# Weight splits rounded in two halves, the second output slab's split moved behind the differential attention, first scores in the free accumulator pair, one join's squares moved ahead

## The reference, cut to what matters

```python
log_a = jax.nn.log_sigmoid((ar @ w_a2 + b_a)) / GLA_TAU
oa = gla(aq, ak, av, log_a)
oa = rmsnorm(oa, gla_gain) * jax.nn.silu(ag)
bq, bk = rmsnorm(bq, dq_gain), rmsnorm(bk, dk_gain)
ob = diff_attention(bq, bk, bv, lam)      # (softmax(q1 k1') - lam softmax(q2 k2')) v, causal
ob = rmsnorm(ob, diff_gain) * (1.0 - lambda_init)
x = x + concat(oa, ob) @ w_out
x = x + conv_ffn(rmsnorm(x, g), w_up, conv_w, conv_b, w_down)
```

## Time and profile before

| | us |
|---|---|
| median of 3 runs | 3355.73 |
| lowest, highest | 3351.95, 3360.63 |
| the profiled execution's own time | 3357.11 |
| its span in the trace | 3355.3 |
| PE busy in the span | 3278.1 (98%) |
| DVE, ACT, POOL busy | 1809.4 (54%), 1247.2 (37%), 1020.4 (30%) |
| granted TensorE clock, mean | 0.995 |

### The profile page before, as it was taken

The page is one execution under the profiler, slowest core; times in us unless marked ns, Lnnn a source line. Parts: engine busy times, 40 slices in busy tenths (PEclk is TensorE's granted clock), DMA queues, the critical chain, the costliest instruction groups (busy, mean ns, idle before and its releaser), DMA issues.

```text
span 3355.3 us, 48284 instructions
## 1 busy us (share of the span) xinstructions
PE 3278.1 (98%) x17840; PEld 2804.2 (84%) x17840; DVE 1809.4 (54%) x2219; ACT 1247.2 (37%) x1627; POOL 1020.4 (30%) x505
## 2 busy tenths in 40 slices
PE   7989999999999999999999999999999999999999
PEld 6768888888888888998888877988888888998887
DVE  5467876553478766457645665664552255262222
ACT  4464333354444334443322445322242223442221
POOL 2112222221112222544434241343423332223332
PEclk9999999999999999999999999999999999999999
DMA  4202333321224333445544310454422243222222
GB/s 143 73 37 101 144 138 125 113 102 51 88 84 156 136 133 109 174 174 185 186 155 175 120 67 14 156 189 150 169 101 100 93 164 113 95 82 100 100 89 100
DMA packets 69901, 401.69 MB, mean 120 GB/s; under 512 B 7520, under 2 KB 10224, under 8 KB 31216
## 3 DMA queue, kind: packets, MB, share of 16 engines
q1 hardware_dynamic: 46400, 317.80, 26.2%
q10 hardware_dynamic: 23344, 81.73, 6.9%
HBM read 397.41 MB, written 2.10 MB: 119 GB/s over the span
## 4 chain that ended last, share of the span: by engine, by line
PE 90%; DVE 3%; ACT 3%; issue 2%; POOL 1%; DMA 1%; SPq 0%; DVEq 0%; ACTq 0%; POOLq 0%
PE banks L535 24%; PE banks L537 23%; PE banks L536 23%; PE banks L441 3%; PE banks L442 3%; PE banks L443 3%; PE banks L552 2%; PE banks L554 2%; PE banks L553 2%; ACT whi L970 1%; POOL wlo L2262 1%; PE banks L651 1%; DMA raw<-stream 1%; PE banks L886 1%; PE banks L873 1%
## 5 line engine op out<-in xcount | busy, mean ns | idle before, releaser
L2262 POOL TENSOR_TENSOR wlo<-raw,whi 128x512 fp32r<-128x512 f32 (+1 forms) x282 | 707.7, 2510 | 2025.7 <-ACT whi L970 2023.7
L535 PE MATMUL banks<-h_hi,whi 128*128 128x512 f32 (+1 forms) x2752 | 1040.2, 378 | 11.5 <-POOL wlo L2262 5.4
L536 PE MATMUL banks<-h_lo,whi 128*128 128x512 f32 (+1 forms) x2752 | 1034.2, 376 | 0.0
L537 PE MATMUL banks<-h_hi,wlo 128*128 128x512 f32 (+1 forms) x2752 | 1034.2, 376 | 0.0
L970 ACT ACTIVATE whi<-raw 128x2048 fp32r<-128x2048 f32 x281 | 536.9, 1911 | 527.8 <-PE banks L537 523.1
L1524 DVE TENSOR_TENSOR wlo<-raw,whi 128x1536 fp32r<-128x1536 f32 (+1 forms) x281 | 530.6, 1888 | 296.2 <-ACT whi L970 296.0
L535 PEld LDWEIGHTS banks<-h_hi,whi 128*128 128x128 f32 x2752 | 518.3, 188 | 112.2 <-issue 16.3
L536 PEld LDWEIGHTS banks<-h_lo,whi 128*128 128x128 f32 x2752 | 518.5, 188 | 94.3 <-issue 1.7
L537 PEld LDWEIGHTS banks<-h_hi,wlo 128*128 128x128 f32 x2752 | 518.5, 188 | 94.0
L535 PE MATMUL banks<-mid_hi,whi 128*128 128x512 f32 (+1 forms) x1136 | 424.6, 374 | 4.0 <-POOL wlo L2262 3.1
L536 PE MATMUL banks<-mid_lo,whi 128*128 128x512 f32 (+1 forms) x1136 | 424.0, 373 | 0.0
(11 more groups left out here) (287 smaller groups left out, 4029.6 us busy)
## 6 DMA issues: line engine op xcount, KB each, us to landing
raw<-stream SPq DMA_DIRECT2D x298, 1024.0 KB, 4.8
mraw<-mod_stream ACTq DMA_DIRECT2D x144, 512.0 KB, 3.4
x<-xT SPq DMA_DIRECT2D x8, 256.0 KB, 6.1
out<-x SPq DMA_DIRECT2D x8, 256.0 KB, 2.2
ka<-k_a ACTq DMA_DIRECT2D x1, 1600.0 KB, 8.6
ko<-k_odd ACTq DMA_DIRECT2D x1, 1152.0 KB, 5.3
crow<-c_rows ACTq DMA_DIRECT2D x1, 1024.0 KB, 7.1
cx<-ctxT SPq DMA_DIRECT2D x1, 1024.0 KB, 7.5
```

Of the source, the lines that this page charges most:

```text
L535: mm(o, hi, a_hi[:, kc, 0:T], start=(kc == 0), stop=False)
L536: mm(o, hi, a_lo[:, kc, 0:T], start=False, stop=False)
L537: last = mm(o, lo, a_hi[:, kc, 0:T], start=False, stop=(kc == K - 1))
L2262: G.tensor_tensor(wlo[:, slot, wd:], raw[:, slot, wd:], whi[:, slot, wd:].bitcast(F32), ALU.subtract)\
```

## The change

1. `split_next` and `split_extra` on ACT round 1024 columns at a time, with a semaphore `whi_half` after the first. POOL takes the first 512 columns (256 in `ctx_ffn`) as soon as the first half is rounded; DVE does the rest of the first half, then waits for the second and does its 1024 columns. So there are two instructions where there was one on ACT and on DVE, 281 slabs long.
2. The split of slab 14 stands behind the differential attention: ACT's halves at units 14 and 15, DVE's and POOL's parts after the last unit. The other attentions keep it in their first unit.
3. Scores of unit n go to `acc[(n + last_slab + 1) % 2]`, so the first goes to the pair that the last projection slab doesn't use, and PE waits for the evacuation only behind the first scores. The wait for the GLA norms moves to the first `turn`.
4. The GLA norms run with one more row in flight (squares of row i+2 ahead of the inverse of row i).
5. At the join cffn1 alone, ACT takes squares 6 and 7 ahead of the rounding of the extra slab.
6. `h_lo` of rows 4 to 7 is made by DVE, not POOL. A 128x1 product is written as another operation.

```diff
             def attention(sems, n0, end, scores, nblocks, w_ap, mix, name, last_slab):
                 def score(n):
                     if n >= n0 + 2:
                         pe.wait_ge(sems["probs"], n - 1)
-                    scores(n, acc[n % 2]).then_inc(sems["scores"], 1)
+                    scores(n, acc[(n + last_slab + 1) % 2]).then_inc(sems["scores"], 1)
                 def turn(n):
+                    if n == 0 and name == "even_in":
+                        pe.wait_ge(hn["rstd"], HN["gla"][0] + 4)
...
+                slab_split(last_slab + 1)
                 score(n0)
+                projections_taken(pe, name)
                 score(n0 + 1)
...
@@ ACT
+            def split_next(s, i2=0, halves=(0, 1)):
                 if s + 2 < NSLAB:
                     act.wait_ge(raw_loaded[s % 2], 16 * ((s + 2) // 2 + 1) + 8 * i2)
                     act.wait_ge(slab_done, s + 1 + i2)
-                    A(whi[:, s % 2, :], raw[:, s % 2, :], ACT.Copy).then_inc(whi_done, 1)
+                    if 0 in halves:
+                        A(whi[:, s % 2, 0:HW], raw[:, s % 2, 0:HW], ACT.Copy).then_inc(whi_half, 1)
+                    if 1 in halves:
+                        A(whi[:, s % 2, HW:], raw[:, s % 2, HW:], ACT.Copy).then_inc(whi_done, 1)
...
                 square(norm, 5)
-                split_extra(s0 + 5)
-                square(norm, 6)
-                square(norm, 7)
+                if norm == "cffn1":
+                    square(norm, 6)
+                    square(norm, 7)
+                    split_extra(s0 + 5)
...
             def head_norm(name, srcs, ready):
-                for i in range(cnt + 1):
+                for i in range(cnt + 2):
                     if i < cnt:
                         ready(i)
                         head_square(n0 + i, srcs[i])
-                    if i:
-                        head_inverse(n0 + i - 1)
+                    if i >= 2:
+                        head_inverse(n0 + i - 2)
...
             def diff_after(n):
+                if n >= 14:
+                    split_next(slab_of("even_in", 12), halves=(n - 14,))
...
@@ DVE
             def split_next(s, i2=0):
                 if s + 2 < NSLAB:
+                    dve.wait_ge(whi_half, s + 1 + i2)
+                    dve.wait_ge(slab_done, s + 1 + i2)
+                    w = slice(pool_part(s), HW)
+                    V.tensor_tensor(wlo[:, s % 2, w], raw[:, s % 2, w], whi[:, s % 2, w].bitcast(F32), ALU.subtract)
                     dve.wait_ge(whi_done, s + 3 + i2)
-                    dve.wait_ge(slab_done, s + 1 + i2)
-                    w = slice(0, dve_part(s))
-                    V.tensor_tensor(wlo[:, s % 2, w], raw[:, s % 2, w], whi[:, s % 2, w].bitcast(F32),
+                    V.tensor_tensor(wlo[:, s % 2, HW:], raw[:, s % 2, HW:], whi[:, s % 2, HW:].bitcast(F32),
                                     ALU.subtract).then_inc(wlo_done, 1)
...
-                        link(V.tensor_tensor(small[:, 46:47], small[:, 45:46], small[:, 5:6], ALU.mult))
+                        link(V.scalar_tensor_tensor(out=small[:, 46:47], in0=small[:, 45:46], scalar=small[:, 5:6],
+                                                    in1=ones[:, 0:1], op0=ALU.mult, op1=ALU.mult))
...
-                    if n == n0:
+                    if n == n0 and ncomp == 1:
                         split_next(last_slab)
...
             attention(sem_diff, 0, 16, 2, dtmp[0], dtmp[1], lambda n: DIFF_U[n][1] + 1, lambda n: None,
                       slab_of("even_in", 12))
-            dve.wait_ge(sem_diff["taken"], 4)
+            split_next(slab_of("even_in", 12))
...
+            def diff_lo(j):
+                dve.wait_ge(hi_done, n0 + 5 + j)
+                V.tensor_tensor(h_lo[:, 4 + j, :], stg[:, (n0 + j) % 2, :], h_hi[:, 4 + j, :].bitcast(F32),
+                                ALU.subtract).then_inc(lo_done, 1)
             for j in range(4):
+                dve.wait_ge(sem_diff["taken"], j + 1)
                 head_out("diff", j, bq[:, j, :], small[:, 6:7], bq[:, j, :])
...
+                if j:
+                    diff_lo(j - 1)
+            diff_lo(3)
...
@@ POOL
-            def split_w(slot, whi_at, done_at, wd=WD):
-                pool.wait_ge(whi_done, whi_at)
-                if done_at is not None:
-                    pool.wait_ge(slab_done, done_at)
-                G.tensor_tensor(wlo[:, slot, wd:], raw[:, slot, wd:], whi[:, slot, wd:].bitcast(F32), ALU.subtract)\
+            def split_w(slot, half_at, done_at, wd):
+                pool.wait_ge(whi_half, half_at)
+                pool.wait_ge(slab_done, done_at)
+                G.tensor_tensor(wlo[:, slot, 0:wd], raw[:, slot, 0:wd], whi[:, slot, 0:wd].bitcast(F32), ALU.subtract)\
                     .then_inc(wlo_pool_done, 1)
...
-            splits(slab_of("even_in"), 13)
+            splits(slab_of("even_in"), 12)
...
             split_h("even", first=3, count=1)
-            split_h("even", first=4, count=4)
+            splits(slab_of("even_in", 12), 1)
```

More of the change, by code:

```diff
@@ L79, with pool_part @@
 IN_CLASSES = ("mix1",)
-def dve_part(s):
+def pool_part(s):
     first, count = PLAN["ctx_ffn"]
-    return SLAB - (WPOOL // 2 if first <= s < first + count else WPOOL)
+    return WPOOL // 2 if first <= s < first + count else WPOOL
 def half_cols(norm, row, a):
```

78 lines of the change are left out of this document (43 added, 35 removed).

## The result

The changed kernel takes 3322.62 us (median of four executions, 3321.38 to 3323.36) against 3355.47 before (four, 3351.95 to 3360.63): ratio 0.9902, interval 0.9889 to 0.9914. The forecast was 3332 in 3324 to 3345. Four later executions of the same kernel gave 3323.64 (3320.48 to 3325.74), so I compare the experiments with 3323, the mean of all eight.

A forecast was written before the change was run, and what follows sets the result against it. PE was busy 98% of the span, so only work PE waits for counts. Terms summed to 24.9 us saved, taking the profiled execution's 3357.1 to 3332.2 (3330.8 from the median); forecast 3332, range 3324 to 3345.

The forecast's parts named there:

- the lock rival: All splits: pieces exclude one another in the bad order, each gains 0.1 instead of 0.7 us; 3343 us, chance 0.15.
- the terms of the halves: Splits at joins, context FFN and elsewhere: rounding in halves alone was to save 12.9 us.
- (e): Four joins with six-block slabs (mix1, m01, m10, m11): shorter waits for splits and statistics save 3.7 us (1 to 4.4).
- (h): Context FFN: shorter splits and a norm chain period of 6.25 instead of 6.75 save 8.5 us (2 to 9.5).
- (i): Small waits for splits elsewhere in the kernel: 0.9 us saved.
- (k): Rotary attention: POOL's work gets between DVE's two pieces, first weights come later; a loss, -1.0 us (-2 to 0).
- clock rival: Attention, cffn1, end of context FFN: new idle stretches still draw the half clock; 19.8 us saved, 3337, chance 0.11.
- (a): GLA norms: one more row in flight and the split's gain shorten PE's waits, 1.6 us saved (0.5 to 2.4).
- (b): Start of the differential attention: first turn 4.15 us behind slab 12 instead of 8.25; 4.1 us saved (3 to 5).
- (f): Join cffn1: statistics come 3 us earlier, then a wait of about 1.9; 4.0 us saved (2 to 5).
- (d): End of the differential attention: DVE's `h_lo` instead of POOL's frees the last row's wait; 0.7 us saved.
- (c): First four units of the differential attention: idle stretch before the half clock goes, 1.0 us saved.

The follow-up runs named there:

- the 13 matmuls: Changed kernel with 13 matmuls on rounded operands, output read by nobody, added behind the first scores of the rotary attention: 3322.01 us.

## Why the prediction was wrong, step by step

**The split's mechanism was right.** "I count 0.7 us per split that PE waits for": over all slabs the median from ACT's start to the last piece went from 4.86 to 4.02 us, 0.84. Both bounds were excluded: the lock rival (4.7) and the split without exclusion. The sum of the lock rival was off by 0.5 in the prediction: its changes leave 13.1 us saved, not 13.6.

**The step that failed is how the terms of the halves were sized: from the idle time in rows, and from the longer rows only.** They came to 12.9 and measured 21 in two runs, which is 8 of the 9 us missed. By place these 8 are 2.0 in (e), 1.9 in (h), 2.4 in (i), 1.0 in (k) and 0.8 at the program's start. By cause:

- Idle time is not what a wait costs: 1.9 us over the sixteen waits for POOL (12.3 us of steps for 10.4 of idle time), all of it where the matmuls closed up again. The prediction made the same slip when it took 5.98 us for PE's eight-block slab: that is the distance of 6.73 between two waits less 0.75 of idle time. The 48 matmuls start 0.12 apart, which makes 5.76, and so it is in the changed kernel.
- Waits that I didn't count, some 4 us. In (i), 0.9 was forecast and 3.3 measured: the two waits of 0.70 without a releaser (1.55), 1.0 at the context statistics and behind them, and a wait of 0.67 for ACT's `h_hi` at 2949 that went. At three joins the waits for statistics, 0.2 each in the timeline and so below what I listed, went with the split ahead of them, 0.4 to 0.5 each; this is the larger part of the miss in (e).

In (h) the chain itself was right: a period of 6.12 for 6.25, and the two waits that stay are 0.69 and 1.58 for 0.8 and 1.7. That its second round came out near the forecast has help from the clock, 1.4 us, for which the prediction's clock rival had 1.6.

**(k)** was too pessimistic. POOL's pooling work did get in between (DVE's pieces took 0.68 and 2.28 us where one had taken 2.51), but the first turn came only 0.35 us later behind the first scores (7.87 for 7.52), not 0.8 to 1.5, and behind the attention nothing of it is left; against the second trace of the changed kernel 0.7 is even saved. At full clock it is 85.7 us from the first scores to the first matmul behind with the whole rounding, and 85.8 with the halves (and the 13 matmuls).

**(a)** was too large: 0.9 for 1.6, and 0.74 when undone. The wait for the inverse stayed 0.69. **(b)** and **(f)** were right, also in what came next; **(d)** was 0.3 too small. The first turn comes 4.22 us behind slab 12 (4.2 forecast), and at cffn1 the wait of 1.74 for `h_lo` is the forecast one.

**(c)** rested on one trace of a thing that differs from execution to execution. It gave 2.5 and took 2.4 in the first trace, 1.2 and 0.5 in the second. The clock rival had its mechanism right, new stretches behind waits of 1 to 2.4 us, and its price too high: at cffn1 they cost nothing (0.03 between the two traces of the changed kernel).

**Not in the terms:** 0.8 us at the program's start and 1.6 by the clock behind the rotary attention. The first goes with the halves: it came back as 1.0 with the halves undone, and the halves alone gave 0.6; against the second trace of the changed kernel it is 0.5. The second is left as the clock's chance.

**The signs.** PE's waits for `wlo` (3.7 left), the first turn at 4.2 us and the wait for `h_lo` at cffn1 came as written, and PE's waits fell by 22 us, not by under 15. That the half clock would be gone was true of its old place only.

The range failed because the bounds of the terms were themselves too low: all upper ones together ((a) 2.4, (b) 5, (e) 4.4, (f) 5, (h) 9.5, (k) 0, the others as they were) save 30.3 us, and 33 were saved. What was missing lies mostly in the halves' terms.

**What stays open:** how much of the 7 us of the old score pair is the wait and how much the clock, and by what the clock falls in one execution and not in the next.

## What to carry to other kernels

Price a removed wait of PE by the starts of the matmuls around it, not by the idle time in its row, and expect the surplus only where they will close up again. Take the short waits behind it and those without a releaser into the list. When two engines exclude one another, add up the pieces from the first moment that one can start; the share given to the slower engine is then a loss (1.2 us for 512 columns on POOL, 0.53 on DVE), unless the other is busy with operands in PSUM at that moment (taking POOL's piece away cost 0.55 us at each such place). Before explaining a difference by the clock, profile the same kernel twice.

## What was not expected of the hardware

The granted clock of one program differs between executions at the same place: behind the same wait of 2.40 us it was 0.50 for 3.4 us in one (the wait ended at 223.10) and 1.00 in the other (224.62). All stretches at half but the one at the program's end stand in or close behind waits of PE; the two traces with three waits of 3.1, 2.4 and 2.2 us filled have none. For the first wait five traces bear that out; for the other two it is not shown, since two traces without added matmuls have none there either. Matmuls of 512 columns took 0.25 us each on rounded operands (13 in 3.25) and 0.86 on unrounded ones with 64 rows (14 in 12.0).
